# Moving the overflow branch of a mixture-of-experts layer behind the expert blocks, and giving the first pair of blocks a token table of its own

## The reference

```
x = x + hierarchical_moe(rmsnorm(x, g_ffn[i]), ...)   # 4 groups x 8 experts; the best group, its 2 best experts
ple_gate = sigmoid(rmsnorm(x, g_ple[i]) @ w_ple_gate[i])
x = x + (p[i] @ w_ple[i]) * ple_gate
```

## Time and profile before

| | |
|---|---|
| median of 3 runs | 2473.81 us (2472.18 to 2477.26) |
| profiled execution | 2474.32 us, span of its instructions 2472.4 us |
| TensorE busy | 2280.0 us (92%), mean granted clock 0.972 |
| DVE / ACT / POOL busy | 993.5 / 588.0 / 402.7 us |
| moved by DMA | 402.86 MB, mean 163 GB/s |

### The profile page before, as it was taken

How to read it: one execution, slowest core, us unless ns; L and a number is a source line. 1 busy time by engine, 2 the same in 40 slices (tenths; PEclk the granted TensorE clock), 3 DMA queues, 4 the chain that set the end, 5 groups by cost and what they waited for, 6 DMA issues and landing times. The chain is left out here.

```text
span 2472.4 us, 29130 instructions
## 1 busy us (share of the span) xinstructions
PE 2280.0 (92%) x11792; PEld 1688.7 (68%) x11792; DVE 993.5 (40%) x1701; ACT 588.0 (24%) x1213; POOL 402.7 (16%) x399
## 2 busy tenths in 40 slices
PE   7989999689889989999698979899999999999998
PEld 6666788444447767788554446687767887888887
DVE  5545533311135444643411116455653334322234
ACT  3533301211123342410311113323441002100012
POOL 2011111112211101111111212111101211112111
PEclk9999999799989999999899999899999999999999
DMA  5114436699962202234789994332222333233321
GB/s 159 52 53 107 126 109 250 262 415 421 422 272 77 68 26 71 65 94 146 304 337 422 421 373 148 86 86 71 79 69 73 102 104 97 85 99 98 95 102 69
DMA packets 291897, 402.86 MB, mean 163 GB/s; under 512 B 31534, under 2 KB 230958, under 8 KB 273834
## 3 DMA queue, kind: packets, MB, share of 16 engines
q1 hardware_dynamic: 276000, 372.56, 42.1%
q0 software_dynamic: 10176, 16.81, 1.8%
q10 hardware_dynamic: 5578, 11.51, 1.7%
HBM read 388.98 MB, written 30.15 MB: 170 GB/s over the span
## 5 line engine op out<-in xcount | busy, mean ns | idle before, releaser
L138 PE MATMUL banks<-h_split,w_high 128*128 128x512 f32 x2624 | 825.7, 396 | 2.3 <-PEq L3142 1.7
L138 PEld LDWEIGHTS banks<-h_split,w_high 128*128 128x128 f32 x2624 | 480.9, 188 | 104.3 <-issue 8.2
L190 DVE TENSOR_TENSOR w_low<-w_raw,w_high 128x1024 fp32r<-128x1024 f32 (+1 forms) x264 | 316.8, 1201 | 502.3 <-POOL w_high L179 502.2
L179 POOL CAST w_high<-w_raw 128x1024 fp32r<-128x1024 f32 (+1 forms) x264 | 277.0, 1050 | 1458.9 <-PE banks L138 1334.1
L138 PE MATMUL banks<-h_split,w_low 128*128 128x512 f32 x1312 | 512.1, 390 | 0.0
L138 PEld LDWEIGHTS banks<-h_split,w_low 128*128 128x128 f32 x1312 | 246.2, 188 | 52.3
L138 PE MATMUL banks<-w_high,op_split 128*128 128x512 f32 x736 | 228.5, 390 | 1.4 <-DVE mg_part L1355 1.1
L1950 PE MATMUL banks<-expert_ring,ex_xsT 128*64 128x256 f32 x1472 | 181.6, 403 | 21.6 <-DMA expert_ring<-in_w_exp_up 18.6
L1950 PEld LDWEIGHTS banks<-expert_ring,ex_xsT 128*64 128x64 f32 x1472 | 108.0, 145 | 81.1 <-DMA expert_ring<-in_w_exp_up 20.5
L138 PEld LDWEIGHTS banks<-w_high,op_split 128*128 128x128 f32 x736 | 138.1, 188 | 31.9 <-DVE mg_part L1355 2.4
L138 PE MATMUL banks<-w_low,op_split 128*128 128x512 f32 x368 | 143.2, 389 | 0.0
(11 more groups left out here) (416 smaller groups left out, 2727.8 us busy)
## 6 DMA issues: line engine op xcount, KB each, us to landing
w_raw<-in_w_in SPq DMA_DIRECT2D x142, 512.0 KB, 4.0
expert_ring<-in_w_exp_gate SPq DMA_DIRECT2D x46, 1024.0 KB
expert_ring<-in_w_exp_up SPq DMA_DIRECT2D x46, 1024.0 KB
expert_ring<-in_w_exp_down SPq DMA_DIRECT2D x46, 1024.0 KB, 22.2
w_raw<-in_w_gu SPq DMA_DIRECT2D x44, 512.0 KB, 4.0
region<-in_w_exp_gate SPq DMA_DIRECT2D x20, 1024.0 KB
region<-in_w_exp_up SPq DMA_DIRECT2D x20, 1024.0 KB
region<-in_w_exp_down SPq DMA_DIRECT2D x20, 1024.0 KB, 17.6
```

Source lines behind the costliest of these rows:

```text
L138: last = nc.tensor.matmul(out, left, right, start=(start and n == 0), stop=(stop and n == 2), skip_group_check=True)
L179: self.nc.gpsimd.tensor_copy(self.high[:, i % self.SPLIT, 0:n], self.raw[:, i % self.RAW, 0:n]).then_inc(self.high_ready, 1)
L190: self.nc.vector.tensor_tensor(self.low[:, i % self.SPLIT, 0:n], self.raw[:, i % self.RAW, 0:n], self.high[:, i % self.SPLIT, 0:n].bitcast ...
```

## The change

- The expert blocks 0 to 32 run inside `merge_and_route`'s program block, in a class `Experts`; the end of that block, the register loads and the overflow branch come after them. The block also takes in 6 of the 8 embedding products (`EARLY_PRODUCTS`), the first splits of `w_ple_gate` and the issue of the loads of the result rows. The overflow body, when it runs, loads its weights into slot 2, stores, and loads the result rows again.
- `border` starts with the clearing of semaphores by POOL; all engines wait for `swept` before they go on.
- The first pair of blocks gets its tokens from a table of its own: `next_rank` and `select` on DVE right after the ranks, four products with 2 columns on TensorE, a conversion to `first_token`, and gather 0. The full table follows; gather 1 uses it. SP issues slot 5's weights only after gather 0 has landed.
- The order on TensorE is turn 0, full table, gate/up 0, half table, hidden 0 turned, gate/up 1, down 0, hidden 1 turned, turn 1, down 1, and then the loop. The refills of blocks 6 and 7 are issued as gate/up 6, gate/up 7, down 6, down 7.
- `turn` and `weigh` signal per half. Gathers are issued a pair earlier in POOL's queue. The ranks, tables and halves lie in other PSUM banks (6 and 7). The scratch for dynamic DMA descriptors is set to 4096 bytes.

```diff
         @block.sync
...
             sp.wait_ge(norm.stored, 16 * NT)
+            sp.wait_ge(e.gathered[0], 16)
             expert_loads.issue(sp, 10)
+            for part in (e.load_gate_up, e.load_down):
+                for n in (EXPERT_SLOTS, EXPERT_SLOTS + 1):
+                    part(sp, n, n)
+            for n in range(EXPERT_SLOTS + 2, EXPERTS):
+                e.load(sp, n)
+            sp.wait_ge(spill_ready, 1)
+            for n in range(EXPERTS, e.blocks):
+                e.load(sp, n)
...
+            sp.wait_ge(e.down_done, e.blocks - 2)
+            gate_stream.loads(sp, 0, gate_stream.RAW)
+            e.stored(sp)
+            results.load(sp)
...
         @block.gpsimd
...
             pool.wait_ge(norm.stored, 16 * NT)
+            pool.wait_ge(first_ready, 1)
+            e.gather(pool, 0, last_token, first_token[:])
             pool.wait_ge(token_ready, 2)
...
+            e.gather(pool, 1, last_token)
+            e.pooled(pool, last_token, last_row, row_ready)
+            pool.wait_ge(e.down_done, e.blocks)
+            gate_stream.split_highs(pool, 0, gate_stream.SPLIT)
...
         @block.tensor
...
+            pe.wait_ge(select_ready, 1)
+            for t in range(NT):
+                last = nc.tensor.matmul(k.ps[:, 7, P:P + 2], select[:, t, :, :].rearrange("p b l -> p (b l)"),
+                                        value[:, 2 * t:2 * t + 2], start=(t == 0), stop=(t == NT - 1))
+            last.then_inc(first_tabled, 1)
+            pe.wait_ge(p_taken, 1)
+            e.turn(pe, 0)
             pe.wait_ge(block_token_ready, 1)
...
             last.then_inc(tabled, 1)
+            e.gate_up(pe, 0)
...
             last.then_inc(halved, 1)
+            e.turn_hidden(pe, 0)
+            e.gate_up(pe, 1)
+            e.down(pe, 0)
+            e.turn_hidden(pe, 1)
+            e.turn(pe, 1)
+            pe.wait_ge(row_ready, 1)
+            e.down(pe, 1)
+            e.multiply(pe, 2)
+            pe.wait_ge(p_landed0, 16)
+            pe.wait_ge(p_landed1, 16)
+            for i in range(EARLY_PRODUCTS):
+                wait(pe, embedding.ready, i - 1)
+                embedding.product(i, k.ps[:, i % 2, :]).then_inc(multiplied, 1)
...
         @block.vector
...
+            link(V.scalar_tensor_tensor(out=next_rank[:], in0=neg_ranks[:, :, 0:FIRST_PAIR], scalar=-1.0,
+                                        in1=member[:].bitcast(F32).rearrange("p (t e) -> p t e", t=NT)[:, :, 0:FIRST_PAIR],
+                                        op0=ALU.add, op1=ALU.mult))
+            V.tensor_tensor(select[:], lane_next[:].unsqueeze(1).unsqueeze(1).to_broadcast([P, NT, FIRST_PAIR, LANES]),
+                            next_rank[:].unsqueeze(3).to_broadcast([P, NT, FIRST_PAIR, LANES]), ALU.is_equal).then_inc(select_ready, 1)
...
+            dve.wait_ge(first_tabled, 1)
+            V.tensor_scalar(first_token[:], k.ps[:, 7, P:P + 1], 2.0 * S, None, ALU.add).then_inc(first_ready, 1)
...
             lanes_hot(slice(4, 8))
...
+            e.weigh(dve, 0)
             dve.wait_ge(tabled, 1)
...
+            e.hidden(dve, 0)
+            e.hidden_turned(dve, 0)
             dve.wait_ge(halved, 1)
...
+                                   op1=ALU.add).then_inc(row_ready, 1)
+            e.hidden(dve, 1)
+            e.hidden_turned(dve, 1)
+            e.weigh(dve, 1)
...
+SPILL_SLOTS = (2,)
...
+GATHERS, OUTPUTS = 2, 3
+FIRST_PAIR = 2
+EARLY_PRODUCTS = 6
...
+    def pooled(self, pool, last_token, last_row, row_ready=None):
+        self.gather_next(pool, GATHERS, last_token)
+        if row_ready:
+            pool.wait_ge(row_ready, 1)
+        for n in range(self.blocks):
+            if n == 1:
+                self.gather_next(pool, GATHERS + 1, last_token)
+            elif n and n % 2 == 0:
+                self.gather_next(pool, n // 2 + GATHERS + 1, last_token)
+            self.scatter(pool, n, last_row)
...
 def border(k, sweep, ple, attention):
+    done, swept = sweep
...
+            sp.wait_ge(swept, 1)
             ple[0](sp)
...
+            clear(k, pool, done)
+            pool.sem_inc(swept, 1)
             ple[1](pool)
...
-    nc = bacc.Bacc("TRN2", target_bir_lowering=False, num_devices=1)
+    nc = bacc.Bacc("TRN2", target_bir_lowering=False, num_devices=1, dynamic_dma_scratch_size=4096)
```

More of the change, by code:

```diff
@@ new lines, in spilled_experts @@
+def spilled_experts(k, ctx, tag, tiles, r, layer, xn_rows, y_rows, weights, results):
+    nc = k.nc
+    xs = k.room(ctx, tag + "_xs", [P, GATHERS, D])
+    landed = sems(k, ctx, f"{tag}_gu_landed {tag}_down_landed")
+    e = Experts(k, ctx, tag, (xs, *tiles[1:]), r, layer, EXPERTS, SPILL, xn_rows, y_rows, weights, SPILL_SLOTS, landed)
+    cleared, reloaded = sems(k, ctx, f"{tag}_cleared {tag}_reloaded")
+    def sync(sp):
+        for n in range(e.blocks):
+            e.load(sp, n)
+        e.stored(sp)
+        for t in range(NT):
+            sp.wait_ge(results.landed[t], 16)
+            sp.dma_start(*results.part(t)).then_inc(reloaded, 16)
+        sp.wait_ge(reloaded, 16 * NT)
+    def gpsimd(pool):
+        last_token, last_row = pool.to_reg(S - 1), pool.to_reg(4 * S - 1)
+        for u in range(GATHERS):
+            nc.gpsimd.memset(xs[:, u, :], 0.0).then_inc(cleared, 1)
+        pool.wait_ge(cleared, GATHERS)
+        for q in range(GATHERS):
+            e.gather(pool, q, last_token)
+        e.pooled(pool, last_token, last_row)
+    def tensor(pe):
+        e.turn(pe, 0)
+        e.multiply(pe, 0)
+    def scalar(act):
+        e.activate(act)
+    def vector(dve):
+        e.weigh(dve, 0)
+        e.vectors(dve, 0)
@@ L3156, in _ @@
         def _(pe):
-            moe[2](pe)
+            pe.wait_ge(swept, 1)
             ple[2](pe)
@@ L3162, in _ @@
         def _(act):
-            moe[3](act)
+            act.wait_ge(swept, 1)
             ple[3](act)
@@ L3326, in first_layer @@
         with nc.If(spilled > ALWAYS - EXPERTS), ExitStack() as rest, nc.Block() as block:
-            more = experts(k, rest, rest, "sp", r, i, EXPERTS, SPILL, xn_rows, y_rows, *weights, xs, gathered)
+            more = spilled_experts(k, rest, "sp", tiles, r, i, xn_rows, y_rows, weights, results)
             block.sync(more[0])
```

426 lines of the change are left out of this document (209 added, 217 removed).

## The result

The changed kernel takes 2454.4 us in the median of 4 runs (2451.9 to 2455.16); the kernel before, beside it, 2473.64 (2472.18 to 2477.26). The ratio is 0.9918, 95% interval 0.9901 to 0.9935: 19.2 us faster. The direction was right, the gain was sized at 10.9. Of all executions behind the numbers of this document one stands apart, 7360 us for "before, no branch", and it is in no comparison. The profiled execution took 2454.77 us, span 2452.9, mean granted clock 0.975.

What follows compares the result with a forecast made beforehand. The experts' weight stream was taken to bound the kernel. A front gain of 23.9 us less a tail loss of 13.0 gave 10.9 off 2474.3: 2463.4, or 2463 on the median, range 2455 to 2472.

Steps and rivals of the forecast that it cites:

- What bounds the kernel: Experts: the weight stream at 412 GB/s sets the pace, so an earlier first refill starts the whole stream earlier.
- The front up to the first refill: From router to first refill: the refill goes out 11.7 us earlier in the first layer, 11.2 in the second.
- The first down projection now comes after two gate-and-up loads ... +0.5 a layer: Stream's start: the new load order closes an idle stretch of about half a us, gaining 0.5 a layer.
- block 2 some 4 us later ... it costs up to 4: Stream's start: TensorE's new order delays block 2; queued loads should hide it, otherwise up to 4 us a layer.
- Loss 6.5 a layer: Tail behind the experts: adds and TensorE's owed products end later, costing 6.5 us a layer, bounds 3 and 11.
- The rule on the jump: Branch behind the experts: a jump outside the prefetched window forces a DMA fetch; TensorE's was taken as 5 us.
- the case in which it pays too: Tail: if DVE's jump also needs a fetch, the adds end near 737 and the loss is 7.1, not 6.5.
- the cheap tail: Tail: adds alone bind, full clock for the last products, loss 3 a layer, 2456 us; chance 0.14.
- the front was handed on more than whole: Rival on the stream: late block 2 opens a gap, 4 us a layer, 2471; chance 0.08.
- the scratch: POOL's descriptors, slower rival: waiting for each indirect transfer to land costs 160 us a layer, about 2780; chance 0.05.
- the first rival: Tail eats the front: fetch at its upper bound, clock stays down, loss 11 a layer, 2472 us; chance 0.17.
- Outside the sum: Everything beyond the front, the stream's start and the tail: forecast as unmoved, 0 us.

Runs made afterwards that it cites:

- before, no branch: The kernel before, without the overflow branch (value load, jump and body left out), the block's end and drains kept: 2465.43 us, ratio 0.9968.
- late gathers: The changed kernel, but from the third pair of blocks on tokens are gathered one pair later, as in the kernel before: 2454.47 us.
- one table: The changed kernel without the short table; the first pair's tokens come from the full table and are turned after it: 2458.48 us.
- experiment 4: The old sequence: the changed kernel with plain order of loads and TensorE's order of before for the first three blocks: 2460.14 us, ratio 0.9945.
- eight products: The changed kernel with all eight embedding products ahead of the branch instead of six: 2464.06 us.
- the filling transposes: The changed kernel with eight products ahead of the branch, and TensorE transposing the identity into an unused bank while waiting for the adds: 2461.28 us.
- the kernel without the branch: The changed kernel without the overflow branch (value load, jump and body): 2451.58 us; with transposes of the identity ahead of each tile's transposes, 2451.39 us.

## Why the prediction was right in its direction and wrong in its size

- **What bounds the kernel**: right. The stream sets the pace of the stage, the late gathers show that TensorE's waits in it are free, and a refill that comes earlier moves the stage.
- **The front up to the first refill**: right. 22.9 forecast, 23.8 measured. It has three parts: the branch (3.7 and 4.0, by "before, no branch"), the short table (2.5 and 3.4, by "one table"), and 4.9 and 5.3 between those two kernels. This last part isn't all the block's end with POOL's drain. From `rt_gsel`, TensorE's first turn begins at 19.7 and 18.6 in "before, no branch" and at 17.6 and 17.1 in "one table": 2.2 and 1.5. The wait of 1.5 us between turn and product is gone, since the first half is weighed while the second is turned. And the product took 4.4 and 4.2 us instead of 5.7 and 6.6, partly at the higher clock.
- **"The first down projection now comes after two gate-and-up loads ... +0.5 a layer", and "block 2 some 4 us later ... it costs up to 4"**: the step that failed first. The stretch from the refill to the embedding products became 3.3 and 3.7 shorter, 7.0 in all for 1.0. I looked at what the new order does to block 2 and not at what it does to the slots: TensorE now does both down projections before block 2, so the down half of the second slot is free some 5 us earlier (473.5 against 478.7, experiment 4), and behind it in SyncE's queue stand block 8's gate and up; and block 7's gate and up no longer wait for a down projection. The trace of before shows the room for it: 386 GB/s in the first 48 us where the full stream has 421, and an idle stretch of some 1.4 us near 481 (share 0.36 and 0.92 in the two windows of 2 us from 480 on) that I had put at half a us. "Old sequence" restores 18.3 MB, 4.9 of the 5.3 us that the stream became shorter, and is 5.8 us slower. The loads' order has 1.3 and 1.2 us, TensorE's order 1.0 and 1.5. Another 1.7 us of the first layer is the last block's product, 3.67 us instead of 5.36. It took 3.67 in the first layer and 5.36 in the second in both traces of the changed kernel, and the other way round in others; what decides it is open.
- **"Loss 6.5 a layer"**: the second step that failed, and the larger one. 3.5 and 3.2 were lost. The parts up to TensorE's return were right: the adds start 13.4 us after the first product (13.1 forecast), the jump took 5.37 and 5.08 (5), TensorE is back after 17.6 and 17.3 (17.4). What I mis-sized stands behind it: the two products took 5.9 instead of 7.1, since the clock rose on the way; the sixteen transposes took 1.9 together instead of 2.6; and the warm TensorE gave back 1.8 and 2.1 in the gate's first stretch, not 0.7. 1.2 + 0.7 + 1.1 are the 3.0 between 6.5 and 3.5. In other words the overlap was wrong: I had TensorE's transposes end 3.4 us behind the adds (737.1 against 733.7), and they ended 1.4 and 1.0 behind them, as before (1.2). So the adds, 5.1 us later in both layers, set the tail, and TensorE's debt behind the jump cost 0.2 us at most.
- **The rule on the jump**: by the Trainium skill, page "Runtime: NRT & Kernel Launch", section on instruction fetch mechanics, a jump beyond the prefetched window costs a fetch by DMA. TensorE's rows agree in that it pays (5.37, 5.08); that a fetch is what it waits for, no row shows. The durations go with the load on the DMA engines only by and large: 6.0 to 6.4 us at a share of 1.00, 4.9 to 5.6 at 0.87 to 1.00, 3.3 to 3.8 at 0.05 and less, but 5.08 at 0.40 in the second layer of eight products, where 3.94 was taken at 0.39 with the filling transposes. My 5 was the right size. DVE's jump at the new place took 0.07 us, so the case in which it pays too did not come.
- **Rivals**: the cheap tail (2456, 0.14) was nearest to the result. The tail did not eat the front, the front was handed on more than whole, and the scratch has no effect. No rival had the fuller start of the stream. (The net of the first rival is 0.7 to 1.2 a layer by its own terms, 11.7 and 12.2 less 11; its 2472 stands.)
- **Outside the sum**: +3 us after the second layer, in most kernels with this timing. The forecast took everything beyond the tail as unmoved. What decides whether the clock falls there is open: kernels that come to it within 1 us of each other do and don't have it. That the measurement lies only 0.6 below the range is partly luck: outside the three stretches 4.7 us were lost in the first trace of the changed kernel and 2.3 in the second.
- **The range** ended at 2455 because the cheap tail was combined with the forecast's front; both steps erring at once by 6 us lay outside it.

## What to carry to other kernels

When an order of work is changed ahead of a stream that bounds the stage, list for each slot when its halves come free and what the queue then loads; bytes moved in the first windows behind the refill are the measure, and they tell what a time that varies by 3 us can't. Small work left over behind a jump is not simply a debt: beside a wait that another engine fills, it was free here, and TensorE's clock was up behind it. And before a gain of a few us is put down to an edit, cut the trace at milestones, since here half and more of such gains lay in stretches that the edit did not touch.

## What the runs showed of the hardware that was not expected

- TensorE's jump over code took 3.3 to 3.8 us with the DMA engines idle (share 0.03 to 0.05), 4.9 to 5.6 at a share of 0.87 to 1.00, 6.0 to 6.4 at 1.00; between those 3.52 at 0.20, 3.94 at 0.39 and 5.08 at 0.40. The jumps of the other engines took 0.04 to 0.07.
- With eight products TensorE, busy 1.31, 2.02 and 1.80 us of three windows of 4 us beside the adds, stood at 1.2 GHz (clock 0.50), and the stretch behind took 2.2 us more; transposes that served nothing but to fill the waits removed that (5.02 us to 2.83). In the kernel without the branch such transposes didn't (4.3 to 4.4).
- POOL's descriptor scratch of 4096 bytes instead of the default left scatters at 998 ns and the kernel at a ratio of 0.9995.
- From the issue of a gather of the normed rows to TensorE's work on them it was 4.4 and 3.6 us on free queues, and 7.9 and 7.7 with 3 MB issued ahead of it.
